# Moving weights and activations by 64 bytes in SBUF: a two-layer macaron network in float32r

## The reference

```
h = rms_norm(x, ffn1_norm[i]);  x = x + 0.5 * swiglu(h, w_gate, w_up, w_down)    # 1024 -> 2816 -> 1024
h = rms_norm(x, mix_norm[i]);   x = x + (even_mixer if i % 2 == 0 else odd_mixer)(h)
h = rms_norm(x, ffn2_norm[i]);  x = x + 0.5 * swiglu(h, w_gate, w_up, w_down)
swiglu(x) = (silu(x @ w_gate) * (x @ w_up)) @ w_down
```

## The kernel before

| tile | before | after |
|---|---|---|
| xu_hi / xu_lo | 0 / 64 | 0 / 0 |
| xs_hi, xs_lo in feed-forward phases | 128 | 0 |
| split x in mixers | 128 (xs) | 64 (xm) |
| raw, w_hi, w_lo, a_hi, a_lo | 128 | 64 |
| gu, gw_hi, gw_lo | 192 | 64 |

## Time and profile before

### The profile page before, as it was taken

The page is one execution under the profiler, slowest core; times in us unless marked ns, Lnnn a source line. Parts: engine busy times, 40 slices in busy tenths (PEclk is TensorE's granted clock), DMA queues, the critical chain, the costliest instruction groups (busy, mean ns, idle before and its releaser), DMA issues.

```text
span 1902.8 us, 31445 instructions
## 1 busy us (share of the span) xinstructions
PE 1872.6 (98%) x11916; PEld 1668.0 (88%) x11916; DVE 1458.7 (77%) x2330; ACT 1021.4 (54%) x1640; POOL 194.8 (10%) x251
## 2 busy tenths in 40 slices
PE   7999999999999999999999999999999999999999
PEld 6899899888779899998889989887778789899997
DVE  8879587577679788597877859756989878687684
ACT  7546264477776355364645526455456766364451
POOL 1311010000001011010011101011111001011010
PEclk9999999999999999999999999999999999999999
DMA  7666662211137565563465546166765376565441
GB/s 241 155 200 183 174 167 64 100 67 67 56 111 183 167 169 146 150 173 109 134 170 156 152 143 179 45 165 161 167 153 131 86 200 170 158 183 161 133 112 67
DMA packets 94789, 271.66 MB, mean 143 GB/s; under 512 B 10504, under 2 KB 10760, under 8 KB 94640
## 3 DMA queue, kind: packets, MB, share of 16 engines
q1 hardware_dynamic: 63456, 201.22, 30.7%
q0 software_dynamic: 29232, 64.50, 19.3%
q10 hardware_dynamic: 1952, 3.93, 1.1%
HBM read 223.07 MB, written 2.77 MB: 119 GB/s over the span
## 4 chain that ended last, share of the span: by engine, by line
PE 88%; DVE 7%; ACT 3%; issue 2%; DMA 0%; DVEq 0%; ACTq 0%
PE ps_unit L814 13%; PE ps_unit L815 13%; PE ps_unit L816 13%; PE ps_y L878 6%; PE ps_y L877 6%; PE ps_y L879 6%; PE ps_s L877 4%; PE ps_s L878 4%; PE ps_t L878 4%; PE ps_t L877 4%; PE ps_t L879 4%; PE ps_s L879 4%; PE ps_s L814 1%; DVE cv L2479 1%; PE ps_s L815 1%
## 5 line engine op out<-in xcount | busy, mean ns | idle before, releaser
L1423 ACT ACTIVATE gw_hi<-gu 128x512 fp32r<-128x512 f32 (+1 forms) x400 | 319.0, 799 | 151.5 <-PE ps_s L879 69.3
L1954 DVE TENSOR_TENSOR gw_lo<-gu,gw_hi 128x512 fp32r<-128x512 f32 (+1 forms) x400 | 354.6, 901 | 46.5 <-ACT gw_hi L1423 35.0
L814 PE MATMUL ps_unit<-a_hi,w_hi 128*128 128x512 f32 x892 | 351.0, 394 | 5.4 <-DVE w_lo L1885 2.8
L815 PE MATMUL ps_unit<-a_lo,w_hi 128*128 128x512 f32 x892 | 348.0, 390 | 0.0
L816 PE MATMUL ps_unit<-a_hi,w_lo 128*128 128x512 f32 x845 | 329.2, 390 | 0.0
L1358 ACT ACTIVATE w_hi<-raw 128x1024 fp32r<-128x1024 f32 (+1 forms) x125 | 125.3, 1003 | 305.1 <-PE ps_unit L816 301.4
L814 PEld LDWEIGHTS ps_unit<-a_hi,w_hi 128*128 128x128 f32 x892 | 167.6, 188 | 44.3 <-DVE w_lo L1885 5.1
L2091 DVE TENSOR_TENSOR t<-ps_unit,half 128x512 f32<-128x512 f32 x96 | 66.4, 691 | 172.8 <-PE ps_unit L816 172.4
L815 PEld LDWEIGHTS ps_unit<-a_lo,w_hi 128*128 128x128 f32 x892 | 167.6, 188 | 32.8
L816 PEld LDWEIGHTS ps_unit<-a_hi,w_lo 128*128 128x128 f32 x845 | 158.6, 188 | 33.8
L879 PE MATMUL ps_y<-xu_hi,gw_lo 128*128 128x256 f32 x640 | 180.5, 282 | 0.0
(11 more groups left out here) (324 smaller groups left out, 4648.7 us busy)
## 6 DMA issues: line engine op xcount, KB each, us to landing
gu<-gu_stream_dram SPq DMA_DIRECT2D x176, 512.0 KB, 5.1
raw<-w_stream_dram SPq DMA_DIRECT2D x136, 512.0 KB, 3.3
gu<-gu_stream_dram SPq DMA_DIRECT2D x80, 256.0 KB, 3.0
gu<-gu_stream_dram POOLq DMA_DIRECT2D x80, 256.0 KB, 4.0
gu<-gu POOLq DMA_DIRECT2D x80, 256.0 KB, 3.3
w_lo<-raw POOLq DMA_DIRECT2D x28, 512.0 KB, 4.9
raw<-w_stream_dram SPq DMA_DIRECT2D x32, 384.0 KB, 3.5
w_lo_3rd<-raw POOLq DMA_DIRECT2D x15, 512.0 KB, 4.7
```

Source lines behind the costliest of these rows:

```text
L814: pe.matmul(ps, lhs_hi, rhs_hi, start=first, stop=False)
L815: pe.matmul(ps, lhs_hi, rhs_lo, start=False, stop=False)
L1423: act.activation(gw_hi[:, w, :], src, ACT.Copy).then_inc(gw_hi_done, 1)
L1954: dve.tensor_tensor(gw_lo[:, w, :], src, gw_hi[:, w, :].bitcast(F32), ALU.subtract).then_inc(gw_lo_done, 1)
```

## The change

The two gaps of 64 bytes behind xu_hi and xu_lo go. Each of xs_hi and xs_lo gets a second name for the mixers, xm_hi and xm_lo, which lies 64 bytes higher over the same memory. The small tile hstd moves into a gap there. By this all that follows moves by 128 or 192 bytes. The mixers' products read xm, and ACT and DVE write xm in place of xs in front of a mixer. No instruction, wait or transfer is added or taken away.

```diff
+BANKS = 256
         xu_hi = sb("xu_hi", [P, PAIRS, 3 * TH], F32R)
-        top[0] += HALF_LINE
         xu_lo = sb("xu_lo", [P, PAIRS, 3 * TH], F32R)
-        top[0] += HALF_LINE
         low_top = top[0]
         xt = sb("xt", [P, KT * T])
-        xs_hi = sb("xs_hi", [P, KT, T], F32R)
-        xs_lo = sb("xs_lo", [P, KT, T], F32R)
+        def xs(name):
+            at, top[0] = top[0], top[0] + HALF_LINE
+            return sb(name, [P, KT, T], F32R, at=at), sb(name + "_mix", [P, KT, T], F32R)
+
+        xs_hi, xm_hi = xs("xs_hi")
+        hstd = sb("hstd", [P, 16])
+        top[0] += BANKS - 2 * HALF_LINE
+        xs_lo, xm_lo = xs("xs_lo")
...
-        hstd = sb("hstd", [P, 16])
...
-                return (lambda k: xs_hi[:, k, :]) if hi else (lambda k: xs_lo[:, k, :])
+                return (lambda k: xm_hi[:, k, :]) if hi else (lambda k: xm_lo[:, k, :])
...
-                act.activation(xs_hi[:, d, :], xt_tile(d), ACT.Copy, scale=scale).then_inc(x_hi_done, 1)
+                hi = xs_hi if PHASES[i] == "ffn" else xm_hi
+                act.activation(hi[:, d, :], xt_tile(d), ACT.Copy, scale=scale).then_inc(x_hi_done, 1)
...
-                dve.scalar_tensor_tensor(xs_lo[:, d, :], xt_tile(d), scale, xs_hi[:, d, :].bitcast(F32),
+                hi, lo = (xs_hi, xs_lo) if PHASES[i] == "ffn" else (xm_hi, xm_lo)
+                dve.scalar_tensor_tensor(lo[:, d, :], xt_tile(d), scale, hi[:, d, :].bitcast(F32),
```

## The result

The kernel after takes 1911.7 us at the median (1911.1 to 1912.1) against 1904.4 for the kernel before beside it (1904.0 to 1905.4): 1.0037 times as long, 95% interval 1.0024 to 1.005. It is slower, outside the predicted range, and within 1.3 us of the 1913 that the first rival gave. The span is 1909.9 us, 7.1 longer than before, at the same granted clock of 0.998.

What follows compares the result with a forecast made beforehand. The prediction took PE as the bound: number of matmuls times their pitch. Terms -12.7 - 4.8 + 1.4 - 0.5 = -16.6 us turned the profiled 1904.64 into 1888.0, median 1888.7 us; range 1884 to 1906.

Steps and rivals of the forecast that it cites:

- the first rival: Feed-forward phases' second and third groups, behind down work, stay at 117.8 ns a matmul: +8.1 us, 1913 us, chance 0.13.
- The entry itself changes: Entry behind down work: the last down matmul no longer loads weights at another distance; counted against 117.8 ns staying.
- The one entry with no change of distance, behind the plain tiles, begins in the short beat: Gate/up entry behind the 512-column plain tiles starts at 113.3 ns at once; counted against 117.8 ns staying.
- xu at distance 64: Gate/up matmuls on xu: 2880 of them drop to the 113.3 ns pitch, saving 12.7 us.
- xs no longer disturbed: Gate/up matmuls on xs behind xu and behind down work drop to the 113.3 ns pitch, saving 4.8 us.
- The first phase gives some back: First phase, behind its stall until down work: some 310 matmuls stay at 117.8 ns, 1.4 us not saved.
- Edges of down work: Changes between gate/up and down work: 20 ns saved at each of 24 entries, 0.5 us.
- Down and mixer products: Down and mixer matmuls: tile and weights move together, distance stays 0; taken as 0, bounds 0 and 22.3 us.
- Splits and transfers: DVE's splits and the transfers: moving w costs DVE nothing and no wait grows; no term in the sum.
- A period of 512 bytes: Gate/up: offsets repeat at 512 bytes, not 256; 1889 to 1928 us, most about 1913, chance 0.08.
- Distance is not the cause: Gate/up matmuls on xu: their row step or place sets the pitch, so nothing changes, 1905 us, chance 0.06.

Runs made afterwards that it cites:

- xu_64: The kernel before with only xu_hi and xu_lo moved to distance 64 from the gate/up weights: 1915.5 us, 1.0055 of before.
- nudge: The kernel after with one extra matmul, 256 to 270 columns wide, ahead of each feed-forward phase's second and third group: 1898.5 us, 0.9967 of before.
- nudge_260: The kernel after with an extra 260-column matmul ahead of each feed-forward phase's second and third group, and one in the first phase: 1889.7 us.
- xu_192: The kernel after with only xu_hi and xu_lo put back at distances 192 and 128 from the gate/up weights: 1904.3 us, 0.9999 of before.
- xs_lo_512: The kernel after with xs_lo and xm_lo 256 bytes higher, raw, w and a moving along, gate/up weights staying: 1912.5 us, 1.004 of before.
- all_0: The kernel after with xs and xu at distance 0 from the gate/up weights, the mixers' split x unmoved: 1929.8 us, 1.0131 of before.
- all_128: The kernel after with xs, xu and the mixers' split x at distance 128 from their weights: 1933.8 us, one run.
- kick6: The kernel after with six extra matmuls at distances 192 and 128 ahead of each feed-forward phase's second and third group: 1917.3 us, 1.0069 of before.
- kick12: The kernel after with twelve extra matmuls, copying an earlier xu piece, ahead of each feed-forward phase's second and third group: 1900.0 us, 0.9975 of before.
- all_192: The kernel after with xs, xu and the mixers' split x at distance 192 from their weights: 1917.8 us, one run.
- xu_back: The kernel after with xu put back, but a gap 64 bytes short also moved xs_lo, xm_lo, a and all weights: 1928.9 us, 1.0127 of before.

## Why the prediction was wrong

**The step that failed** is that the sum counts the gains of xu and xs, -17.5 us, and takes back only 1.4 of them, as if the groups behind down work ran in the short beat. This went against the prediction's own first rival, "The long beat stays". That rival's place, price and direction were right: the second and third groups stay long, 117.8 ns through all of their 659 pitches, at 1913 against a measured 1911.7. It had a chance of 0.13 for two reasons, and both fell. "The entry itself changes": the edge did change, down work runs evenly to its end, but the group behind it still begins in the long beat. "The one entry with no change of distance, behind the plain tiles, begins in the short beat": that was one entry, and not a rule; in `xu_64` the same entry with the same distances was long in two phases and short in a third. `nudge` and `nudge_260` show what stands behind both: at distance 64 either beat keeps itself up, and a few columns ahead of the first matmul choose, so no argument from distances alone can tell which.

**"xu at distance 64", -12.7 us, and "xs no longer disturbed", -4.8.** The sizes were right and the condition, "if xu runs in the short beat", was not met behind down work. Where it was, in the first groups of the later phases and in `nudge_260`, xu and xs run at 113.3 ns. `nudge_260` is 14.6 us below before. The sum, -16.6, with nine extra matmuls at some 0.12 us each (1.1 us) gives -15.5; the first phase's first group, 156 matmuls, came out long there, 0.7 us of the rest. What the reading missed is that the disturbance by xu had a use: each tile's xu pieces threw xs out of the long beat, and `xu_64` and `xu_192` show that moving xu alone makes the whole loss and moving it back undoes it. The prediction had said that the xu piece ends the long beat, and still counted only its cost.

**The other terms.** "The first phase gives some back" came near in size by luck: 1.4 us were forecast behind the stall of rows 8, but there the short beat came back. The 168 matmuls that stay long, 0.7 us, lie behind a small matmul of the bias table (onehot, relb) at about 55 us, which cuts the stretch in two and which the prediction passed over. "Edges of down work": saved, 0.5. "Down and mixer products": no loss, 394 and 403 ns as in the earlier trace rows. "Splits and transfers": DVE's busy time is 1458.6 us against 1458.7.

**The other rivals.** A period of 512 bytes fell with `xs_lo_512`. "Distance is not the cause" fell with `all_0`, `all_128` and `xu_192`. The rule of the Trainium skill (TensorE: Matmul & The Clock Gate, Part 2, "Step-by-step"), that loading weights takes nothing from the running matmul's reads, is not borne out here by the pitch: with the same matmuls and clock the place of the moving tiles against the weights gave 113.3 to 120.0 ns. That the two reads meet in the memory is argued from this, not shown.

**What stays open.** Why 64 and 192 have two steady beats, and what the moment is measured against: the runs show that a few columns choose, not what keeps the rhythm. Whether the xu pieces of before bring the short beat back by their distance or by the moment at which they leave the next piece to start is open too, as kick6 and kick12 were not taken apart further.

## What to carry to other kernels

Before an irregularity is smoothed away, ask what it resets: here the dearer pieces were also what brought the others back to the cheaper pace, and one run with only those pieces moved would have told. Where one and the same row of matmuls is seen at two paces, ask what selects the pace at each entry, and count the entries on which the answer rests. If both paces keep themselves up, one odd-sized matmul at each entry may be all it takes: `nudge_260` is 0.9919 of before (0.9905 to 0.9932).

## What the runs showed of the hardware

- The pitch of float32r matmuls of 256 columns, each with its own weights, hangs on the distance of the two offsets within 256 bytes: 120.0 ns at 0, about 118.8 or 120.0 at 128, and 113.3 or 117.8 at 64 and at 192 (128 and 192 from one run each). The mixers' matmuls of 512 columns go another way, by their durations: their dearest form took 403 ns at 0, 405 in `all_192` and 407 in `all_128`; in `xu_back`, with the high part at 192 and the low part at 0, it took 409.
- At 64 both beats lasted through whole groups, 659 pitches, and the width of one extra matmul chose: 256 long, 258 to 262 short, 264 and 266 long, 268 and 270 short, each tried at one entry.
- With 260 columns all eight entries came out short, in a kernel whose time moved from 1911.7 to 1889.7 us by nine matmuls more.
